# The combined projection's weight in contiguous blocks, and a third raw buffer for the gate blocks

## The reference, cut to what matters

```python
h = rmsnorm(x, norm_mix)            # (1032, 1024)
u = h @ w_in                        # (1032, 1024) @ (1024, 2216)
c_q, c_kv, k_r, z, xbc, dt = split(u, [384, 256, 32, 512, 1024, 8])
```

## Time and profile before

| | |
|---|---|
| median of 3 runs | 1567.0 us (1564.93 to 1568.64) |
| profiled execution, its own time | 1567.2 us |
| its span in the profile | 1565.4 us |
| mean granted clock of PE | 0.946 |
| PE busy | 1391.5 us |
| DVE, ACT, POOL busy | 912.3, 664.1, 150.3 us |

### The profile page before, as it was taken

How to read it: one execution, slowest core, us unless ns; L and a number is a source line. 1 busy time by engine, 2 the same in 40 slices (tenths; PEclk the granted TensorE clock), 3 DMA queues, 4 the chain that set the end, 5 groups by cost and what they waited for, 6 DMA issues and landing times. The chain is left out here.

```text
span 1565.4 us, 23215 instructions
## 1 busy us (share of the span) xinstructions
PE 1391.5 (89%) x8147; PEld 1125.6 (72%) x8147; DVE 912.3 (58%) x1368; ACT 664.1 (42%) x952; POOL 150.3 (10%) x245
## 2 busy tenths in 40 slices
PE   4999999798888897987768996499999999978997
PEld 3878999587566676665536885388888888853786
DVE  3331553687566663333325555598899898943563
ACT  4333234331233331221214230487878878834432
POOL 1110000231000001000000010110000000000451
PEclk9999999897899997999989997699999999998999
DMA  7315110352244334356526552579866799935441
GB/s 221 122 55 156 44 52 30 117 143 98 82 107 114 81 93 122 87 163 174 159 64 234 195 201 96 209 273 387 317 215 229 283 396 397 398 126 215 161 162 54
DMA packets 147284, 267.41 MB, mean 171 GB/s; under 512 B 24177, under 2 KB 75890, under 8 KB 146850
## 3 DMA queue, kind: packets, MB, share of 16 engines
q1 hardware_dynamic: 138242, 233.46, 44.6%
q0 software_dynamic: 5760, 20.97, 3.8%
q10 hardware_dynamic: 3168, 11.54, 1.8%
HBM read 215.06 MB, written 50.87 MB: 170 GB/s over the span
## 5 line engine op out<-in xcount | busy, mean ns | idle before, releaser
L2373 DVE TENSOR_TENSOR low_gate<-raw_gate,high_gate 128x2048 fp32r<-128x2048 f32 x44 | 99.3, 2289 | 33.6 <-ACT high_gate L2290 33.6
L2373 DVE TENSOR_TENSOR low_down<-raw_down,high_down 128x2048 fp32r<-128x2048 f32 x44 | 98.8, 2288 | 15.2 <-ACT high_down L2290 15.1
L2373 DVE TENSOR_TENSOR low_up<-raw_up,high_up 128x2048 fp32r<-128x2048 f32 x44 | 98.9, 2287 | 4.9 <-ACT high_up L2290 3.0
L1394 PE MATMUL pb<-cst,pages 128*128 128x128 f32 x512 | 72.8, 306 | 23.3 <-DMA pages<-in_cache 20.0
L2290 ACT CAST high_gate<-raw_gate 128x2048 fp32r<-128x2048 f32 x44 | 82.2, 1909 | 17.3 <-DMA raw_gate<-in_w_gate 17.3
L1394 PEld LDWEIGHTS pb<-cst,pages 128*128 128x128 f32 x512 | 66.2, 159 | 31.5 <-DMA pages<-in_cache 23.8
L514 PE MATMUL pb<-hH,blkH 128*128 128x344 f32 x264 | 84.6, 320 | 0.0
L2290 ACT CAST high_up<-raw_up 128x2048 fp32r<-128x2048 f32 x44 | 82.4, 1923 | 4.9 <-SPq L2150 3.9
L515 PE MATMUL pb<-hL,blkH 128*128 128x344 f32 x264 | 84.4, 320 | 0.0
L516 PE MATMUL pb<-hH,blkL 128*128 128x344 f32 x264 | 84.4, 320 | 0.0
L1563 DVE COPY pgT<-pb 128x512 f32<-128x512 f32 x64 | 41.8, 687 | 72.2 <-PE pb L1394 71.7
(11 more groups left out here) (430 smaller groups left out, 3434.2 us busy)
## 6 DMA issues: line engine op xcount, KB each, us to landing
pages<-in_cache SPq DMA_DIRECT2D x256, 144.0 KB, 2.4
raw_gate<-in_w_gate SPq DMA_DIRECT2D x32, 1024.0 KB, 9.7
raw_up<-in_w_up SPq DMA_DIRECT2D x32, 1024.0 KB, 10.6
raw_down<-in_w_down SPq DMA_DIRECT2D x32, 1024.0 KB, 8.8
y_d<-yo ACTq DMA_DIRECT2D x22, 512.0 KB, 6.3
raw<-in_w_in SPq DMA_DIRECT2D x17, 512.0 KB, 4.3
y_d<-zero SPq DMA_DIRECT2D x16, 512.0 KB, 4.5
xt<-in_x_all SPq DMA_DIRECT2D x9, 512.0 KB, 5.7
```

The costliest lines, as they stand in the source:

```text
L1394: last = pe.transpose(pb[:, g, (2 * c + half) * P:(2 * c + half + 1) * P], pages[b % 3][:, 8 * m + 4 * half + g, c * P:(c + 1) * P], ident)
L2373: dve.tensor_tensor(part(low_[w], c), part(raw[w], c), part(high[w], c).bitcast(F32), ALU.subtract).then_inc(S(w + "_low"), 1)
```

## The change

On the host, `w_in` is laid out anew. `w_blk` holds the 17 blocks of 128 columns, each as 128 partitions of 1024 contiguous numbers (8 k by 128 columns), in the order of their use; `w_kd` holds the 40 columns of block 2 as 128 partitions of 320. Block 2 is now one load. A third raw buffer `rawA` takes block 3 and then block 6: `RAW_AT` gives blocks 0 to 6 the buffers 0, 1, (own), 2, 0, 1, 2, and from block 7 on 0 and 1 in turn. Hence the waits: blocks 0 to 3 wait for nothing, 4 and 5 for the low halves of blocks 0 and 1, 6 for that of block 3, 7 and 8 for those of 4 and 5, and all later ones as before. Block 3 is issued ahead of `brow`.

```diff
+        rawA = sb_in(p1a, "rawA", [P, KD, P])
...
-            return n // 2 + (1 if n % 2 or n == 0 else 0)
+            return RAW_AT[:n + 1].count(RAW_AT[n])
...
+        RAW_AT = [0, 1, None, 2, 0, 1, 2] + [n % 2 for n in range(CT + 3)]
...
-            return raw[n % 2][:, :, :]
+            return (rawA if RAW_AT[n] == 2 else raw[RAW_AT[n]])[:, :, :]
...
             def load_raw(n):
-                if n == 3:
-                    sp.wait_ge(S("rawL_rdy"), 2)
-                elif n > 3:
+                if 4 <= n <= 5:
+                    sp.wait_ge(S("rawL_rdy"), n - 3)
+                elif 6 <= n < NBLK + 2:
+                    sp.wait_ge(S("rawL_rdy"), n - 2)
+                elif n >= NBLK + 2:
                     sp.wait_ge(S("rawL_rdy"), n - 1)
-                a, w = RAWS[n]
-                if a is None:
-                    sp.dma_start(raw_of(n)[:, :, 0:ROPE], wv[:, :, C_KR:C_Z]).then_inc(S("kd_in"), 16)
-                    sp.dma_start(raw_of(n)[:, :, ROPE:w], wv[:, :, C_DT:IN_COLS]).then_inc(S("kd_in"), 16)
+                if n == 2:
+                    sp.dma_start(raw_of(n), t_in["w_kd"].rearrange("p (k n) -> p k n", k=KD)).then_inc(S("kd_in"), 16)
                 else:
-                    sp.dma_start(raw_of(n), wv[:, :, a:a + w]).then_inc(S(f"raw_in{n % 2}"), 16)
+                    sp.dma_start(raw_of(n), t_in["w_blk"][n - (n > 2), :, :].rearrange("p (k n) -> p k n", k=KD)).then_inc(S(f"raw_in{raw_at(n)}"), 16)
...
-            load_raw(0)
-            load_raw(2)
-            load_raw(1)
+            for n in (0, 2, 1):
+                load_raw(n)
             load_x(1)
+            load_raw(3)
             sp.dma_start(brow[:, :], t_in["brow"]).then_inc(const_in, 16)
-            load_raw(3)
             load_raw(4)
...
+    w_in = f["w_in"][0].reshape(KD, P, IN_COLS).transpose(1, 0, 2)
+    starts = ([C_CKV, C_CKV + P] + [C_Z + P * m for m in range(4)] + [C_X + P * c for c in (4, 5, 6, 7, 0, 1, 2, 3)] + [P * m for m in range(3)])
...
-        "w_in": f["w_in"][0],
+        "w_blk": np.stack([w_in[:, :, a:a + P].reshape(P, -1) for a in starts]),
+        "w_kd": np.concatenate([w_in[:, :, C_KR:C_Z], w_in[:, :, C_DT:IN_COLS]], 2).reshape(P, -1),
```

More of the change, by code:

```diff
@@ L79, in program @@
         "x_all", "p_t", "cache", "page_table", "conv_prev", "ssm_prev")]
-    w_in, w_uq, w_ukv, w_ukt, w_out, w_rout = [t_in[n] for n in ("w_in", "w_uq", "w_ukv", "w_ukt", "w_out", "w_rout")]
+    w_uq, w_ukv, w_ukt, w_out, w_rout = [t_in[n] for n in ("w_uq", "w_ukv", "w_ukt", "w_out", "w_rout")]
     def scratch(name, shape, dt=F32):
@@ L265, in raw_low, with raw_at @@
             return wzL[:, :, (n - 3) * P:(n - 2) * P] if n < NBLK else blkL[(n - NBLK) % 2][:, :, :]
+        RAW_AT = [0, 1, None, 2, 0, 1, 2] + [n % 2 for n in range(CT + 3)]
+        def raw_at(n):
+            return RAW_AT[n]
         def raw_of(n):
@@ L293, in _ @@
         def _(sp):
-            wv = w_in.rearrange("(k p) n -> p k n", p=P)
             def load_x(i):
@@ L703, in split_high @@
                 if n == 2:
-                    act.wait_ge(S("kd_in"), 32)
+                    act.wait_ge(S("kd_in"), 16)
                 else:
-                    act.wait_ge(S(f"raw_in{n % 2}"), 16 * raw_count(n))
+                    act.wait_ge(S(f"raw_in{raw_at(n)}"), 16 * raw_count(n))
                 if NBLK <= n < NBLK + 2:
```

## The result

The changed kernel takes 1558.8 us (median of 7 runs, 1556.5 to 1561.6) against 1567.0; the ratio is 0.9950, with a 95% interval of 0.9939 to 0.9961, so 6 to 10 us less. Forecast were 1557.7 us, 9.3 us less, with a range of 1555 to 1563. The profiled execution took 1561.6 us, at the slow end of its runs, with a span of 1559.9: 5.5 us less than the span before.

The account below looks back on a forecast made before the run. PE bounds the kernel, so its 7.8 us wait before the first gate rows counts: gate rows 7.67 us earlier plus 1.66 us from the clock make 9.3 us, giving 1557.7 us on the median, range 1555 to 1563.

Parts of the forecast that it names:

- Rate of a block: Gate weight block loads: 4096-byte rows move at 411 GB/s instead of 320, a block taking 1.28 us instead of 1.64.
- Rival A: Block loads: the new rows bring no rate; gate rows 5.5 us earlier, 1561.5 us in all; chance 0.13.
- Small rows: Block 2's key/step-size rows (L309): one load, issue 0.43 us instead of 3.57, and the slow 2.1 us stretch goes.
- rival D: SP queue: each new load costs 3.57 us to issue, gate rows 4.4 us late, 1571.4 us; chance 0.04.
- Landing times: Prologue loads land in issue order at 411 GB/s after gmix at 6.95: block 1 at 9.90, block 6 at 20.54.
- The wait added: Block 6's load waits for block 3's low half on DVE until 16.8; with 3.7 us landing, it arrives at 20.5.
- both roads meet: Block 6's landing: queue order and the wait for block 3's low half both give 20.5 us.
- The clock: Gate rows' 24 matmuls run at the upper clock level, 5.62 us instead of 7.28, adding 1.66 us of gain.
- PE is at work again sooner than that after its last instruction: PE's wait before the gate rows: 3.0 us instead of 7.8, ending before the clock falls.
- Rival B: Gate rows: the clock falls all the same in the remaining 3 us; 7.67 us gained, 1559.3 us; chance 0.15.
- Blocks 7 to 17 and the rest: Later blocks: PE waits for none of them, hidden behind 11.3 us of products each, so faster rows gain nothing.
- Rival C: Behind the gate rows: a stage ending by something that doesn't move gives the gain back, 1567 us; chance 0.08.

Follow-up runs that it names:

- No waits: Against the changed kernel: blocks 4, 5 into the empty key/value weight tile, block 6 into raw buffer 0, all ahead of brow, x tile 2, constants; 1556.6 us, ratio 0.9931.
- small rows alone: The kernel before with only block 2's small rows re-laid and loaded in one; 512-byte block rows and two buffers kept; ratio 0.9988 to the kernel before.
- PE kept busy: The changed kernel with 28 extra matmuls, read by nothing, on PE before the first gate rows; ratio 0.9953 to the kernel before.
- Constants later: The changed kernel with tile 2 of x, cols and the rest of cst issued behind blocks 5 and 6; ratio 0.9948 to the kernel before.
- buffer alone: The changed kernel's third buffer, waits and order, but blocks as 512-byte rows and small rows in two loads; ratio 0.9986 to the kernel before.
- Old rows: The changed kernel with only the block rows put back to 512 bytes, block 2 still in one load; ratio 0.9974 to the kernel before.

## Why the prediction was right

The mechanism held: the gate rows' start moved, everything behind it moved by as much, and block 6 remained the last to arrive. The size was 9.3 us forecast, and 5.5 and 7.5 us in the two profiles' spans, 8 and 7 us in the two sets of timed runs. So it was 1 to 4 us too large, and that the median of 1558.8 came within 1.1 us of 1557.7 is in part luck. Its terms, with the two profiles of the changed kernel:

| term | forecast | first | second |
|---|---|---|---|
| DVE starts on `gmix` | 6.95 | 7.77 | 7.96 |
| from there to block 1 on ACT | 2.95 | 3.01 | 3.01 |
| block 1 to block 4 | 5.48 | 6.58 | 5.48 |
| block 4 to block 5 | 3.89 | 3.97 | 4.15 |
| block 5 to block 6 | 1.27 | 1.26 | 1.42 |
| block 6 to gate rows | 2.36 | 2.36 | 2.36 |
| gate rows start | 22.90 | 24.95 | 24.38 |
| 24 gate matmuls | 5.62 | 7.26 | 5.67 |

```profile
DMA packets 604, 1.76 MB, mean 352 GB/s; under 512 B 190, under 2 KB 190, under 8 KB 604
```

```profile
DMA packets 613, 1.76 MB, mean 352 GB/s; under 512 B 197, under 2 KB 197, under 8 KB 613
```

- *Rate of a block*: right. 411 GB/s taken, 419 measured from 7.5 to 13 us, where the new rows move together with `x` and `brow`, and 2.2 us for six blocks against 1.7 to 2.3 (issue included). Rival A was rightly given little.
- *Small rows*: right in what they cost, not in every sign: block 3's issue took 0.95 us in the first profile and 1.12 in the second, where under 0.5 was forecast and over 1 was to speak for D. The other new loads took 0.33 to 0.45, and the gate rows came earlier, so rival D falls. That `cprev`'s 3.01 us were those of a full queue holds: in "No waits", where SP had stood still for 6 us ahead of `wkv`, the same load took 0.65 us. The small rows alone gave 1.7 us (28.72 against 30.4).
- *Landing times*: the term that was mis-sized. It hung on one number of one execution, `gmix` at 6.95, which lands between 6.8 and 8.0 from one execution to the next; this is 0.8 to 1.0 of the 1.5 to 2.0 us that the gate rows are late. The other 1.1 us in the first profile stand between blocks 1 and 4. They are absent in the second, and in "PE kept busy" and "Constants later", with the same queue up to block 4, it is 5.45 and 5.41 us where 5.48 was forecast. The rate doesn't explain it: from 13 to 18 us both profiles moved 352 GB/s (lines above, first and second), under the 411 that were taken. Why block 4 was late in the first stays open.
- *The wait added*: right, 17.6 against 16.8 for the issue of block 6, the same 0.8 us of `gmix`. But "both roads meet" didn't hold: in the first profile block 6 landed 5.0 us after its issue, not 3.7, and 1.26 behind block 5. So the queue was the later road, by 1.3 us (0.6 in the second profile). With the constants out of its way it took 3.64 us ("Constants later").
- *The clock*: right in one of two profiles. The step "PE is at work again sooner than that after its last instruction" was a weak one: it took the distance at which the clock fell in one profile for one that holds in all. In the first profile PE stood still for 4.2 us and the clock fell, in the second for 2.8 and it didn't. That these 2.8 are near the forecast 3.0 is luck: the gate rows were 1.5 us late, and PE, slower at the start, was free 1.7 us late. Rival B, 1559.3, is what the first profile came to in mechanism, with a chance of 0.15 that was too low.
- *Blocks 7 to 17 and the rest*: right as far as can be told. Rival C, which gives all the gain back, would lengthen the distance from `turn_c` to the end by some 8 us; it is 1527.7 and 1527.8 us, against 1525.4 to 1527.55 in the three profiles before. A change of 2 us or less there can't be seen.

## What to carry to other kernels

When a load of a prologue is late, write down what stands before it in its queue and which buffer it waits for; here the rows of the blocks, the small rows and the buffer each moved the gate rows by some 2 us, and taking the remaining waits away (blocks parked in a tile that is still empty) gave 3.3 us more in the medians for no work at all. Landing times taken from one execution carry an uncertainty of a microsecond at the start of a kernel, which a forecast of a few microseconds has to hold in its range. Transfers whose rows are joined to 4 KB were worth a host-side layout here although the rows already had 512 bytes.

## What the runs showed of the hardware

The fall of the granted clock doesn't keep a fixed distance from PE's last work. In the first profile of the kernel before PE ended at 22.80 and the fall lies at 27.2; in its second PE ended at 22.83 and the clock had fallen by 25 (row below); with the small rows alone PE ended at 22.37 and the fall lies in the row from 24 to 25. Twice it came as PE was starting again: at 25.0 in the changed kernel, and at 28.2 with the buffer alone, 5.0 us after PE's end at 23.21 (second row). With the constants later, PE stood still for 2.3 us, longer than the 2.0 after which it fell in the second profile before, and the clock stayed at 1.00.

```profile
24.00:25.00 1.00, 0.00 (x0) 0.00 (x0) 0.00 (x0) 0.02 (x1) 0.00 (x0) 0.91 0.89 178
```

```profile
28.00:29.00 1.00, 1.00 (x3) 0.80 (x4) 0.46 (x3) 1.00 (x3) 0.55 (x1) 0.61 1.13 299
```

An issue on SP is no fixed cost either: behind more than 1000 small rows the same L309 took 3.57, 2.96 and 4.05 us in three profiles of the kernel before, and the loads of the new rows 0.33 to 1.12 us in two profiles of the changed kernel. Here it went by what stood in front more than by the load itself: 128 rows of `x` took 3.76 us behind two blocks of 1024 rows ("Old rows"), and `cprev` 3.07 us in the changed kernel but 0.65 with "No waits":

```profile
20.61 0.65 SPq L346 DMA_DIRECT2D cprev<-in_conv_prev  x1
```
